# Residual kept in PSUM, norm scale applied to the gathered rows, one weight lent rows, fewer warm-up matmuls, last down weights by columns

## The chip, the core and the metric

The kernel runs on one core of a Trainium2 chip (trn2): TensorE (PE, with a separate weight-load stream PEld), VectorE (DVE), ScalarE (ACT), GpSimd (POOL), the queue of SyncE (SP) that issues nearly all transfers, and 16 DMA engines. The metric is the device time of one execution in microseconds; lower is better.

## What is computed

A trunk of two layers for 256 tokens of 1024 channels, all in float32. Layer 0 mixes by attention, layer 1 by a gated linear recurrence; behind each mixer stands a mixture of 32 SwiGLU experts, and a norm ends the trunk. Cut to what matters:

```python
for layer in range(2):
    h = h + mixer(rms_norm(h, norm_mix[layer]))
    x = rms_norm(h, norm_ffn[layer])
    # top-1 of 4 groups, then top-2 of the group's 8 experts; combine[s, e] is the weight or 0
    hid = silu(einsum('sd,edf->sef', x, w_gate)) * einsum('sd,edf->sef', x, w_up)
    h = h + einsum('sef,efd->sd', hid * combine[..., None], w_down)
return rms_norm(h, final_norm)
```

All 32 experts of a layer are computed, each on the tokens that chose it, so that 3 x 32 weight matrices of 1 MB are read in each layer.

## The kernel before

**Tiles.** The tokens are two row tiles t of 128. `h` is [128, 2, 1024] in SBUF, `xg` and `xT` are as large, `psum` has 8 banks of 512 floats. Weights lie in `ring` (6 slots of 16 KB a partition), in the `arena`, in `ahead`, and in rows lent for a time (`gain`, `xT`'s upper half as `y_rows`).

**Expert stage.** The experts go in 8 quads of 4. Every quad has at most 32 tokens an expert, so a quad fills the 128 columns of a matmul, each expert its own 32. For quad n TensorE does, in this order, in `body`: `gather` (16 matmuls, `xg` times the 0/1 matrix `slots`, so the chosen tokens come out transposed), `combine` of quad n-2 (4 matmuls of 512 columns that bring the quad's outputs back to the token rows, times `shareT`), `turn_hidden` of n-1, `later_gate_up` of n (32 matmuls; the four experts of a step run side by side), `down` of n-1 (16 matmuls) and `turn_shares`. ACT and DVE copy the gathered rows out of PSUM (ACT the front half in four pieces, DVE the back half, L1558), compute silu, and copy the down product to `y_rows`. DVE adds the four banks of each combine to `h` (`add_rows`, L1549). ACT writes `xg` as h times the norm's `rstd` once per layer (`scaled_rows`). Quad 0 uses pieces of its gate/up weights (`first_gate_up`, four pieces c) as they come; the first lies between the two halves of the gather.

**Transfers.** SP issues them in program order and stands at each wait. `later_quad(n, q, parity, ended)` waits until gate/up of quad n-2 is done (its slots are free), issues the 8 gate and up matrices of quad q, waits for the down product of quad n-2 and issues the 4 down matrices of the quad `ended`. So quad 3's eight loads (L500) wait for gate/up of quad 1, and quad 2's down loads (L508) for the down product of quad 1 and everything ahead of it on TensorE. The last quad's down weights (`load_last_down`, L541) come in four transfers: row half j = 0 of both slots, then j = 1.

**Ends.** Behind the last quad, ACT squares h by halves (`norm_by_halves`), DVE norms both tiles (L1246), and in layer 0 the transposes, the split in high and low parts and the products of the recurrence follow; in layer 1 two stores do. At the start `keep_clock(16, 7)` issues 16 matmuls on the identity (L1816), the gain row is spread by two matmuls (L1822), eight more follow, and then come the norm's transposes (L1798).

## Time and profile before

| | us |
|---|---|
| median of 3 runs | 728.1 |
| lowest, highest | 727.38, 729.61 |
| the profiled execution | 732.78 |
| its span, first to last instruction | 731.1 |
| TensorE busy in it | 624.0 (85%) |
| DVE, ACT busy in it | 300.8, 242.6 |
| moved by DMA | 244.52 MB, mean 334 GB/s |

The span is a little shorter than its execution's time. Busy shares are means over stages that differ: the slices and windows show them apart. In a timeline row the columns are start, duration, engine, line, operation, out and in tiles, shape, count of records, and in brackets the idle time ahead and what ended it. A float32 matmul shows as two records (a transpose as one), and its records overlap, so that the start-to-start distance tells the pace.

### The profile page before, as it was taken

To read this page: it belongs to the slowest core of one execution; us is meant where nothing else is said; L and a number is where in the kernel's file an instruction comes from. 1 tells how busy PE (TensorE), PEld (TensorE's weight loads), DVE (VectorE), ACT (ScalarE), POOL (GpSimd) and SP (SyncE) were. 2 spreads that over 40 slices of the span, in tenths; PEclk is the share of its full clock that TensorE was granted. 3 is DMA by queue.
4 is the path that set the end of the run, shared out by engine and by line. 5 is a ranking of instruction groups with operands and counts; after the bars stand their busy time and mean duration, and the time that the engine had idled before them with its cause. 6 is when DMAs were issued, how large, how long until landed. Compare 5 with 4: busy or idle time off the path is not lost.

```text
span 731.1 us, 11097 instructions
## 1 busy us (share of the span) xinstructions
PE 624.0 (85%) x4490; PEld 411.3 (56%) x4490; DVE 300.8 (41%) x518; ACT 242.6 (33%) x540; POOL 35.2 (5%) x64
## 2 busy tenths in 40 slices
PE   8999899999997595675989999999999976595775
PEld 7997787776542341322269987887754431341321
DVE  3756687524232211312285698652522330221304
ACT  4545556442211110100157685662411110110112
POOL 3020000000000100000000001060000000000000
PEclk9999999999999888977999999999999998897989
DMA  8949336799999999999996636579989999999993
GB/s 325 274 123 340 114 117 208 306 403 360 401 422 392 410 420 421 421 422 422 405 388 220 231 128 218 185 265 403 386 358 392 416 422 422 422 421 421 421 415 142
DMA packets 59712, 244.52 MB, mean 334 GB/s; under 512 B 4545, under 2 KB 8913, under 8 KB 38930
## 3 DMA queue, kind: packets, MB, share of 16 engines
q1 hardware_dynamic: 58400, 242.33, 84.5%
q0 software_dynamic: 768, 1.40, 0.8%
q8 instruction: 31, 0.51, 0.3%
q10 hardware_dynamic: 498, 0.15, 0.1%
q14 instruction: 15, 0.12, 0.0%
HBM read 242.82 MB, written 1.05 MB: 334 GB/s over the span
## 4 chain that ended last, share of the span: by engine, by line
PE 54%; DMA 31%; DVE 5%; SPq 5%; ACT 2%; issue 2%; DVEq 0%; POOL 0%; POOLq 0%; ACTq 0%
DMA ring<-in_moe_w_down 31%; PE psum L2278 7%; PE psum L1849 6%; PE psum L2223 6%; PE psum L1860 3%; PE psum L1853 3%; SPq L541 3%; PE psum L1851 3%; PE psum L1858 3%; PE psum L2216 3%; PE psum L2358 2%; PE psum L2360 2%; PE psum L2359 2%; SPq L508 2%; PE psum L1816 1%
## 5 line engine op out<-in xcount | busy, mean ns | idle before, releaser
L2223 PE MATMUL psum<-ring,xT 128*32 128x512 f32 x512 | 66.9, 679 | 33.5 <-DMA ring<-in_moe_w_up 33.5
L2223 PE MATMUL psum<-arena,xT 128*32 128x512 f32 x512 | 63.9, 657 | 34.6 <-DMA arena<-in_moe_w_up 34.6
L1567 DVE TENSOR_TENSOR arena<-psum,arena 128x256 f32<-128x256 f32 x16 | 6.8, 425 | 210.3 <-ACT arena L1051 210.3
L2278 PE MATMUL psum<-ring,arena 128*32 128x512 f32 x456 | 61.8, 626 | 14.4 <-DMA ring<-in_moe_w_down 14.3
L1047 ACT ACTIVATE arena<-psum 128x256 f32<-128x256 f32 x16 | 6.1, 383 | 202.0 <-PE psum L2223 202.0
L2216 PE MATMUL psum<-arena,xg 128*128 128x128 f32 x512 | 61.5, 277 | 0.8 <-DVE arena L1553 0.8
L2216 PEld LDWEIGHTS psum<-arena,xg 128*128 128x128 f32 x512 | 59.3, 193 | 2.7 <-issue 2.7
L2223 PEld LDWEIGHTS psum<-arena,xT 128*32 128x32 f32 x512 | 16.9, 120 | 76.8 <-issue 41.2
L2223 PEld LDWEIGHTS psum<-ring,xT 128*32 128x32 f32 x512 | 16.9, 123 | 76.0 <-issue 41.1
L2207 PE MATMUL psum<-xT,arena 128*128 128x512 f32 x128 | 57.7, 594 | 0.0
L1849 PE MATMUL psum<-x_hi,w_hi 128*128 128x256 f32 x224 | 56.0, 288 | 1.7 <-DVE x_hi L1252 1.2
L1549 DVE TENSOR_TENSOR h<-psum,h 128x512 f32<-128x512 f32 x64 | 44.2, 690 | 9.3 <-PE psum L2207 8.2
L1853 PE MATMUL psum<-x_hi,w_lo 128*128 128x256 f32 x192 | 47.0, 283 | 0.0
L2278 PEld LDWEIGHTS psum<-ring,arena 128*32 128x32 f32 x456 | 15.6, 114 | 53.3 <-issue 36.1
L1849 PEld LDWEIGHTS psum<-x_hi,w_hi 128*128 128x128 f32 x224 | 42.7, 191 | 3.6 <-issue 1.8
L835 ACT ACTIVATE w_hi<-ring 128x1024 fp32r<-128x1024 f32 x32 | 32.7, 1052 | 18.7 <-PE psum L1860 11.6
L2207 PEld LDWEIGHTS psum<-xT,arena 128*128 128x128 f32 x128 | 23.1, 190 | 24.6 <-issue 24.6
L410 DVE TENSOR_TENSOR w_lo<-ring,w_hi 128x1024 fp32r<-128x1024 f32 x28 | 33.3, 1220 | 8.5 <-ACT w_hi L835 8.5
L1853 PEld LDWEIGHTS psum<-x_hi,w_lo 128*128 128x128 f32 x192 | 36.7, 191 | 0.0
L1860 PE MATMUL psum<-x_lo,w_hi 128*128 128x256 f32 x224 | 31.5, 283 | 0.1
L1558 DVE TENSOR_TENSOR xT<-psum,gain_ffn 128x512 f32<-128x512 f32 x16 | 11.1, 692 | 46.3 <-PE psum L2216 46.3
L1040 ACT ACTIVATE xT<-psum,gain_ffn 128x128 f32<-128x128 f32 x64 | 18.5, 367 | 31.8 <-PE psum L2216 31.8
(341 smaller groups left out, 1050.2 us busy)
## 6 DMA issues: line engine op xcount, KB each, us to landing
ring<-in_moe_w_down SPq DMA_DIRECT2D x54, 1024.0 KB, 20.1
ring<-in_moe_w_gate SPq DMA_DIRECT2D x32, 1024.0 KB, 15.5
ring<-in_moe_w_up SPq DMA_DIRECT2D x32, 1024.0 KB, 17.7
arena<-in_moe_w_gate SPq DMA_DIRECT2D x32, 1024.0 KB, 20.7
arena<-in_moe_w_up SPq DMA_DIRECT2D x32, 1024.0 KB, 22.6
ring<-in_rec_w_in SPq DMA_DIRECT2D x16, 1024.0 KB, 13.7
ring<-in_att_w_in SPq DMA_DIRECT2D x8, 1024.0 KB, 10.7
ring<-in_att_w_out SPq DMA_DIRECT2D x4, 1024.0 KB, 14.7
```

Source lines behind the costliest of these rows:

```text
L410: eng.tensor_tensor(quarter_lo(base, r), quarter(base, r), quarter_hi(r).bitcast(F32), ALU.subtract)\
L541: sp.dma_start(slot.rearrange("p (e j n) -> p e j n", e=2, j=KF)[:, :, j, :], v[j][:, 2 * i:2 * i + 2, :])\
L835: act.activation(quarter_hi(r), quarter(base, r), ACT.Copy).then_inc(s["w_high"], 1)
L1549: dve.tensor_tensor(v, bank(b), v, ALU.add).then_inc(done, 1)
L1849: pe.matmul(dst, a_hi(k), b_hi(k), start=(k == 0), stop=False)
L1851: pe.matmul(dst, a_hi(k), b_lo(k), start=False, stop=False)
L1853: pe.matmul(dst, a_lo(k), b_hi(k), start=False, stop=False)
L1860: last = pe.matmul(dst, a_hi(k), b_lo(k), start=False, stop=(k == KD - 1))
L2207: pe.matmul(bank(b), shareT[:, t, :], y_rows[:, half * 512:(half + 1) * 512], start=True, stop=True).then_inc(s[f"combined{l}"], 1)
L2216: last = pe.matmul(gather_bank(k, first)[:, k % 4 * P:(k % 4 + 1) * P], xg_parts[:, t, k, :], slots[:, t].rearrange("p e c -> p (e c)"), s ...
L2223: return pe.matmul(bank(3)[e * CAP:(e + 1) * CAP, :].rearrange("p (w f) -> p w f", w=2), gatheredT[:, k, e * CAP:(e + 1) * CAP], w, start= ...
L2278: last = pe.matmul(bank(5 + c)[e * CAP:(e + 1) * CAP, :], hidT[:, j, e * CAP:(e + 1) * CAP], down_part(l, kind, e, j)[:, c * 512:(c + 1) * ...
```

## The change

1. **Sums in PSUM.** `combine` accumulates in banks 0 to 3 over all quads; DVE's `add_rows` is gone. In the body of quad 2 `start_sums` first writes h there, by four matmuls with the identity. The working banks move to 4 to 7. At the layer's end norm and squares read PSUM; in layer 0 h is copied back to SBUF later.
2. **Scale after the gather.** `scaled_rows` is gone; `gather` reads h itself, with a step of 8 floats, and adds two matmuls of one column that gather `rstd`. ACT copies that column negated (`slot_rate`), and silu uses it as a scale.
3. **Lent rows.** `xg` is free during the stage, so the gate matrix of quad 2's expert 0 is loaded there during the mixer (`load_in_x`); its expert's product is split in two matmuls of 256 columns.
4. **Quad 0** does pieces 0 and 1 of gate/up between the halves of the gather.
5. **Warm-up.** `START, FIRST` go from 16, 4 to 6, 2; the identity is made before the ones.
6. **Last quad.** Its down weights come in eight transfers, by column half and then row half; TensorE takes them in that order, and combines the front columns ahead of the last piece.
7. **Between the layers** the small lower-bound work moves ahead of the last down product; the first product of the recurrence takes its three parts one after the other; the last store is in two halves.

```diff
+LAST_PARTS = ((0, 0, "last_down_front"), (0, 1, "last_down_front"), (1, 0, "rest_loaded"), (1, 1, "last_down_back"))
...
+        def load_in_x(sp, l, *free):
+            sp.wait_ge(*free)
+            sp.dma_start(x_weights, moe_w_gate[l].rearrange("(q e) (p r) f -> q e p (r f)", e=QE, p=P)[2][0])\
+                .then_inc(s[f"gate_up_loaded{l}_0"], 16)
...
-            for j in range(KF):
+            for c, j, done in LAST_PARTS:
                 for i, slot in enumerate(down_slots(l, True)):
-                    sp.dma_start(slot.rearrange("p (e j n) -> p e j n", e=2, j=KF)[:, :, j, :],
-                                 v[j][:, 2 * i:2 * i + 2, :])\
-                        .then_inc(s["last_down_back" if j else "last_down_front"], 16)
+                    sp.dma_start(slot.rearrange("p (e j n) -> p e j n", e=2, j=KF)[:, :, j, c * 512:(c + 1) * 512],
+                                 v[j][:, 2 * i:2 * i + 2, c * 512:(c + 1) * 512]).then_inc(s[done], 16)
...
                     load_lent(sp, 0, 0, s["xg_done"], TT)
+                    load_in_x(sp, 0, s["proj_psum"], 12)
...
-                    load_gate_up(sp, l, 2, 0, e)
+                    load_gate_up(sp, l, 2, 0, e, (0, 1) if e else (1,))
...
-        START, FIRST, ROUTE, NORM = 16, 4, 19, 10
+        START, FIRST, ROUTE, NORM = 6, 2, 19, 10
...
+            def slot_rate(l, n, parity, small=False):
+                act.wait_ge(s[f"rate_psum{l}"], n + 1)
+                act.activation(rate[:, parity:parity + 1], rate_psum(small), ACT.Copy, scale=-1.0)\
+                    .then_inc(s[f"gatheredT{l}"], 1)
...
-            def add_rows(l, m, done):
-                dve.wait_ge(s[f"added{l}"], 4 * m + 4)
-                for i, b in enumerate(COMBINE_BANKS):
-                    half, t = divmod(i, 2)
-                    v = h[:, t, half * 512:(half + 1) * 512]
-                    dve.wait_ge(s[f"combined{l}"], 4 * m + i + 1)
-                    dve.tensor_tensor(v, bank(b), v, ALU.add).then_inc(done, 1)
...
+            def start_sums(l):
+                for done in (f"y_front{l}", f"y_back{l}", "passes_ready"):
+                    pe.wait_ge(s[done], l + 1 if done == "passes_ready" else 1)
+                for half, t in SUM_TILES:
+                    pe.matmul(sum_bank(half, t), ident[:, :], h[:, t, half * 512:(half + 1) * 512],
+                              start=True, stop=False, skip_group_check=True)
...
-                    pe.matmul(bank(b), shareT[:, t, :], y_rows[:, half * 512:(half + 1) * 512],
-                              start=True, stop=True).then_inc(s[f"combined{l}"], 1)
+                    pe.matmul(sum_bank(half, t), shareT[:, t, :], y_rows[:, half * 512:(half + 1) * 512],
+                              start=False, stop=last, skip_group_check=True)\
+                        .then_inc(s["h_done" if last else f"combined{l}"], 1)
...
+                    if k == KD - 1:
+                        for t in range(TT):
+                            col = pe.matmul(rate_psum(small), slots[:, t].rearrange("p e c -> p (e c)"),
+                                            norm_rstd[:, v, t:t + 1], start=(t == 0), stop=(t == TT - 1))
+                        col.then_inc(s[f"rate_psum{l}"], 1)
...
+                        if in_x and e == 0:
+                            for i, part in enumerate((lent, w[0][:, 1])):
+                                pe.matmul(bank(GATE_UP)[0:CAP, i * FF:(i + 1) * FF], gatheredT[:, k, 0:CAP],
+                                          part[:, k, :], start=(k == 0 and i == 0), stop=(k == KD - 1),
+                                          skip_group_check=True)
...
-                down(l, end, last_quad=True)
-                pe.wait_ge(s[f"added{l}"], 4 * end + 4)
-                combine(l, end)
+                last_down(l, 0, 0)
+                last_down(l, 0, 1)
+                last_down(l, 1, 0)
+                combine(l, end, last=True, halves=(0,))
+                last_down(l, 1, 1)
+                combine(l, end, last=True, halves=(1,))
```

How TensorE's instructions stand, at three places. **Quad 0 of layer 0**, before; `arena` is `slots` (and hidden rows), `xT` the gathered tokens, `ring` the weights:

```order
L2216 MATMUL psum<-arena,xg 128x128 [waits slots0,route_exp,xg_done]
L2216 MATMUL psum<-arena,xg 128x128 x7
L2223 MATMUL psum<-ring,xT 32x512 [waits first_loaded0,first_front]
L2223 MATMUL psum<-ring,xT 32x512 x7
L2216 MATMUL psum<-arena,xg 128x128 x8
L2223 MATMUL psum<-ring,xT 32x512 [waits first_loaded1,first_front]
L2223 MATMUL psum<-ring,xT 32x512 x7
L2223 MATMUL psum<-ring,xT 32x512 [waits first_loaded2,gatheredT0]
L2223 MATMUL psum<-ring,xT 32x512 x7
L2223 MATMUL psum<-ring,xT 32x512 [waits first_loaded3,gatheredT0]
L2223 MATMUL psum<-ring,xT 32x512 x7
```

and after:

```order
L2276 MATMUL psum<-arena,h 128x128 [waits slots0,route_exp,norm_rstd]
L2276 MATMUL psum<-arena,h 128x128 x7
L2284 MATMUL psum<-ring,xT 32x512 [waits first_loaded0,first_front]
L2284 MATMUL psum<-ring,xT 32x512 x7
L2284 MATMUL psum<-ring,xT 32x512 [waits first_loaded1,first_front]
L2284 MATMUL psum<-ring,xT 32x512 x7
L2276 MATMUL psum<-arena,h 128x128 x6
L2272 MATMUL psum<-norm_rstd,arena 128x1 x2
L2276 MATMUL psum<-arena,h 128x128 x2
L2284 MATMUL psum<-ring,xT 32x512 [waits first_loaded2,gatheredT0]
L2284 MATMUL psum<-ring,xT 32x512 x7
L2284 MATMUL psum<-ring,xT 32x512 [waits first_loaded3,gatheredT0]
```

The second pair of gate/up rows now stands ahead of the gather's back half, and two matmuls on `norm_rstd` inside that half. **The body of quad 2 of layer 0**, from the gather to the start of gate/up, before:

```order
L2216 MATMUL psum<-arena,xg 128x128 [waits slots0,added0]
L2216 MATMUL psum<-arena,xg 128x128 x15
L2207 MATMUL psum<-xT,arena 128x512 [waits y_front0,shareT0]
L2207 MATMUL psum<-xT,arena 128x512
L2207 MATMUL psum<-xT,arena 128x512 [waits gatheredT0,y_back0]
L2207 MATMUL psum<-xT,arena 128x512
L2258 MATMUL psum<-ident,arena 128x128 [waits hid0]
L2258 MATMUL psum<-ident,arena 128x128
L2223 MATMUL psum<-ring,xT 32x512 [waits gate_up_loaded0_0,gatheredT0]
L2223 MATMUL psum<-ring,xT 32x512 x31
```

and after (the last two rows and three of 512 columns on `ring` behind them come eight times):

```order
L2276 MATMUL psum<-arena,h 128x128 [waits slots0]
L2276 MATMUL psum<-arena,h 128x128 x13
L2272 MATMUL psum<-norm_rstd,arena 128x1 x2
L2276 MATMUL psum<-arena,h 128x128 x2
L2243 MATMUL psum<-h,ident 128x512 [waits passes_ready,y_back0,y_front0]
L2243 MATMUL psum<-h,ident 128x512 x3
L2257 MATMUL psum<-xT,arena 128x512 [waits y_front0,shareT0]
L2257 MATMUL psum<-xT,arena 128x512
L2257 MATMUL psum<-xT,arena 128x512 [waits gatheredT0,y_back0]
L2257 MATMUL psum<-xT,arena 128x512
L2310 MATMUL psum<-xg,xT 32x256 [waits gate_up_loaded0_0,gatheredT0]
L2310 MATMUL psum<-ring,xT 32x256
```

The four matmuls on `h,ident` are new between gather and combine, and the rows of expert 0 are two of 256 columns. **The last quad of layer 0**, from its down product on, before:

```order
L2278 MATMUL psum<-ring,arena 32x512 [waits last_down_front,hidT0]
L2278 MATMUL psum<-ring,arena 32x512 x7
L2278 MATMUL psum<-ring,arena 32x512 [waits last_down_back]
L2278 MATMUL psum<-ring,arena 32x512 x7
L2322 REGISTER_ALU
L2207 MATMUL psum<-xT,arena 128x512 [waits y_front0,shareT0,added0]
L2207 MATMUL psum<-xT,arena 128x512
L2207 MATMUL psum<-xT,arena 128x512 [waits y_back0]
L2207 MATMUL psum<-xT,arena 128x512
L1816 MATMUL psum<-ident 128x128 x10
```

and after:

```order
L2398 MATMUL psum<-ident,chosen 128x16 [waits lb_loaded]
L2334 MATMUL psum<-ring,arena 32x512 [waits last_down_front,hidT0]
L2334 MATMUL psum<-ring,arena 32x512 x3
L2334 MATMUL psum<-ring,arena 32x512 [waits last_down_front]
L2334 MATMUL psum<-ring,arena 32x512 x3
L2334 MATMUL psum<-ring,arena 32x512 [waits rest_loaded]
L2334 MATMUL psum<-ring,arena 32x512 x3
L2257 MATMUL psum<-xT,arena 128x512 [waits y_front0,shareT0]
L2257 MATMUL psum<-xT,arena 128x512
L2334 MATMUL psum<-ring,arena 32x512 [waits last_down_back]
L2334 MATMUL psum<-ring,arena 32x512 x3
L2257 MATMUL psum<-xT,arena 128x512 [waits y_back0,shareT0]
```

The product is in four pieces with a wait each, the front columns are combined ahead of the last piece, and the lower-bound transpose stands ahead of all.

## Rows read from the trace of the kernel before

**Rows 1.** The page's 40 slices of 18.3 us: TensorE's busy tenths, GB/s moved.
```profile
PE   8999899999997595675989999999999976595775
...
GB/s 325 274 123 340 114 117 208 306 403 360 401 422 392 410 420 421 421 422 422 405 388 220 231 128 218 185 265 403 386 358 392 416 422 422 422 421 421 421 415 142
```

**Rows 2.** The page's chain that ended last, by line, share of the span.
```profile
DMA ring<-in_moe_w_down 31%; PE psum L2278 7%; PE psum L1849 6%; PE psum L2223 6%; PE psum L1860 3%; PE psum L1853 3%; SPq L541 3%; PE psum L1851 3%; PE psum L1858 3%; PE psum L2216 3%; PE psum L2358 2%; PE psum L2360 2%; PE psum L2359 2%; SPq L508 2%; PE psum L1816 1%
```

**Rows 3.** Windows: stretch, length, busy us (count) by engine, PEclk, DMA share, GB/s.
```profile
135.20:140.20 5.00, 4.35 (x31) 3.15 (x30) 1.45 (x3) 2.94 (x4) 0.00 (x0) 1.00 0.14 38
...
197.20:197.80 0.60, 0.60 (x8) 0.60 (x7) 0.02 (x1) 0.57 (x3) 0.00 (x0) 1.00 0.70 232
...
197.80:216.00 18.20, 18.20 (x144) 8.75 (x144) 7.00 (x13) 4.04 (x11) 1.16 (x2) 1.00 1.00 414
...
529.20:532.20 3.00, 3.00 (x26) 1.45 (x19) 0.00 (x0) 0.00 (x0) 0.00 (x0) 0.84 0.21 41
...
555.00:573.00 18.00, 18.00 (x142) 8.55 (x142) 6.80 (x13) 3.84 (x11) 0.58 (x1) 1.00 0.99 412
```

**Rows 4.** Timeline of SP's DMA issues: start, us, line, what is loaded.
```profile
124.67 0.43 SPq L534 DMA_DIRECT2D gain<-in_moe_w_down  x1
...
196.62 0.35 SPq L500 DMA_DIRECT2D arena<-in_moe_w_gate  x1
...
214.64 1.88 SPq L508 DMA_DIRECT2D ring<-in_moe_w_down  x4
...
553.64 0.34 SPq L500 DMA_DIRECT2D arena<-in_moe_w_gate  x1
...
571.65 1.88 SPq L508 DMA_DIRECT2D ring<-in_moe_w_down  x4
```

**Rows 5.** Timeline, layer 0: transposes of h, counts, an eviction, gather, combine.
```profile
158.85 2.04 PE L1808 MATMUL psum<-ident,h 128*128 128x128 f32 x16
...
169.18 0.39 PE L2193 MATMUL psum<-member,ones 128*128 128x32 f32 x2
...
169.40 0.39 PE L2194 MATMUL psum<-member,ones 128*128 128x32 f32 x2
...
176.18 0.69 DVE L1558 TENSOR_TENSOR xT<-psum,gain_ffn 128x512 f32<-128x512 f32 x1 [2.75 <-PE psum L2216]
...
196.60 3.74 PE L2216 MATMUL psum<-arena,xg 128*128 128x128 f32 x32
...
200.18 3.60 PE L2207 MATMUL psum<-xT,arena 128*128 128x512 f32 x8
```

**Rows 6.** Timeline of the kernel's start.
```profile
1.86 6.72 PE L1816 MATMUL psum<-ident 128*128 128x128 f32 x32 [1.86 <-POOL eps_col L713]
...
8.51 1.98 PE L1822 MATMUL psum<-gain,ones 1*128 1x512 f32 x4
...
10.61 2.47 DVE L1240 SCALAR_TENSOR_TENSOR xg<-h,norm_rstd,psum 128x1024 f32<-128x1024 f32 x2 [10.61 <-PE psum L1822]
...
17.11 2.17 PE L1874 MATMUL psum<-x_hi,w_hi 128*128 128x256 f32 x16 [0.35 <-ACT w_hi L937]
```

**Rows 7.** Timeline, end of layer 0 (one row), then of layer 1.
```profile
371.80 2.48 DVE L1246 SCALAR_TENSOR_TENSOR xg<-h,norm_rstd,gain 128x1024 f32<-128x1024 f32 x2 [0.94 <-ACT norm_rstd L826]
...
715.65 1.92 PE L2278 MATMUL psum<-ring,arena 128*32 128x512 f32 x16
...
718.17 1.92 PE L2278 MATMUL psum<-ring,arena 128*32 128x512 f32 x16 [0.59 <-DMA ring<-in_moe_w_down]
...
719.30 0.60 ACT L1065 ACTIVATE xT<-psum 128x512 f32<-128x512 f32 x1 [3.16 <-PE psum L2278]
...
720.04 3.68 PE L2207 MATMUL psum<-xT,arena 128*128 128x512 f32 x8
...
724.07 0.63 ACT L814 ACTIVATE arena<-h 128x512 f32<-128x512 f32 x1
...
725.39 2.48 DVE L1246 SCALAR_TENSOR_TENSOR xg<-h,norm_rstd,gain 128x1024 f32<-128x1024 f32 x2 [0.94 <-ACT norm_rstd L826]
```

285 lines of the change are left out of this document (166 added, 119 removed).

## Prediction

> **What bounds the kernel now.** I read the 40 slices of the page first, then the chain that ended last, then the DMA share in windows of my own, then the timelines of the queue SP and of TensorE. The slices show two regimes [rows 1]: TensorE is at 9 tenths or more through both mixers and the first part of each expert stage, and from about 200 us (and again from about 550 us) the 16 DMA engines are at 9 tenths with about 420 GB/s while TensorE falls to 5 to 7 tenths. The chain agrees: 31% of the span is spent waiting for the down weights [rows 2]. The expert stages are therefore a race in which the transfers win in the end, and what counts is the moment from which the transfers never stop. The windows give that moment [rows 3]: the DMA share is 1.00 from 197.8 us in layer 0 and 0.99 from 555 us in layer 1, and the slices behind stay at some 420 GB/s [rows 1]. Before it there are holes: 135.2 to 140.2 (share 0.14), 197.2 to 197.8 (0.70), and 529.2 to 532.2 (0.21). From that moment on the end of a layer is fixed by bytes alone.
>
> What starts the last stretch is TensorE. The eight transfers of quad 3 are issued at 196.62 (553.64 in layer 1) as soon as the gate/up product of quad 1 is finished, and the down weights of quad 2 at 214.64 (571.65) as soon as the down product of quad 1 is finished [rows 4]. TensorE has no idle between the two: it is busy for 18.2 of the 18.2 us of that window [rows 3], with gather, combine [rows 5], gate/up and down back to back. Eight transfers are 8 x 1.05 MB = 8.4 MB; at the 414 GB/s of [rows 3] they take 20.3 us and run from 197.8 to 218.1. The next issue at 214.64 brings data some 1.3 us later (196.62 to 197.8 and 553.64 to 555.0 are the same delay), at 215.9. **So TensorE has 2.1 us of slack in layer 0**, and in layer 1, where data flow from 555.0 to 575.3 and the issue at 571.65 brings data at 573.0, 2.3 us. Whatever the change adds on TensorE before the end of quad 1's down product, beyond that slack, delays the layer's end one for one.
>
> **The change part by part.**
>
> *Work added on TensorE before that point.* (a) Each gather now carries two matmuls of one column. None is in the trace; the nearest rows are the count matmuls of 32 columns, 0.22 us from start to start (169.18 to 169.40), paced by their weight loads. Lower bound 0.1, upper 0.25 us each; I take 0.22, so 0.44 per gather and 1.3 us for the three gathers (0, 1, 2) before the point. (b) In quad 0 the second piece of gate/up moves ahead of the back half of the gather. DVE's eviction of that half (0.69 us [rows 5], starting 0.2 to 0.3 after the gather's end) was hidden behind that piece; now the third piece waits for it: about 0.95 us. (c) Before the sums, h is put in PSUM by four matmuls with 512 columns. Four such matmuls are the combine, 3.60 us for its eight records, 0.86 from start to start [rows 5]: 3.4 us. They stand between gather 2 and combine 0, where nothing was idle, so nothing hides them. (d) Quad 2's expert 0 is split in two matmuls of 256 columns, eight times. The columns are the same; experts run side by side. If only the pipeline skews, this costs one half step, 0.4 us; if every extra start held up the other experts it would cost 3.4 us; nothing in the trace has mixed widths. I take 0.4, because four experts overlap fully in every gate/up row. Sum: 1.3 + 0.95 + 3.4 + 0.4 = 6.1 us, minus the slack: **+4.0 us in layer 0 and +3.8 us in layer 1.** What is queued behind it is the SP queue: it stands at the wait for quad 1's down product and has 12 transfers behind that wait.
>
> *The lent rows.* One gate weight (1 MB, 2.5 us of transfer) is now issued behind the last transfer of its group at 124.67 [rows 4] and flows in the hole at 135.2 to 140.2 [rows 3], which is 5 us long; in layer 1 it moves likewise into mixer time. It costs nothing there. But it gains nothing either: it shortens the queue before the issue of quad 3, and that issue waits for TensorE. The queue runs dry at about 194.7 instead of 197.2 and idles longer. The bytes after the point are the same.
>
> *What is removed.* ACT's scaled copies (2.2 and 2.4 us) and DVE's four adds of 0.69 us per quad leave engines that are idle for half of these stages: worth nothing until the last quad. The extra waits on y_front and y_back before a gather are met: the copies end before TensorE has turned the shares. The small extra ACT instruction (0.2 us) is covered by combine.
>
> *Short warm-up.* Before, 32 warm-up records take 6.72 us (0.21 each, the lower clock), then the gain matmuls run from 8.51, DVE's first norm starts at 10.61, released by them and by nothing later, and the first product at 17.11 [rows 6]. With 6 instead of 16 the warm-up ends at about 4.1, the gain matmuls (1.98 us at the upper, twice that at the lower clock) end at about 8.0, so the norms start 2.5 us earlier, and the 8 warm-up matmuls that held back the transposes become 3. Against it: the transposes may run at the lower clock throughout (0.21 instead of 0.13 us each [rows 5, 6]). I take -2.4 us, with bounds -3.2 and -0.5 (the lower clock until the first products have run for some microseconds). The mixer is a chain of compute with holes in the DMA, so the shift arrives at the expert stage.
>
> *End of layer 0.* The sum stays in PSUM, the last down product comes by columns. TensorE is nearly the bound here. From 715.65 in layer 1 [rows 7] (layer 0 ends in the same pattern): three pieces of 0.86 us to 718.2; ACT copies the first half of the rows 1.13 us after the start of its second piece (718.17 to 719.30) in 0.60, so until 718.3; two combine matmuls to 720.1; the last piece, its copy, and combine at 722.0; the result 1.15 us later, the square and rstd 1.3 us (724.07 to 725.39), first final norm at 724.5. Before it was 725.39. So 0.9 us, although the last transfer now is followed by only a quarter of the product: TensorE itself is late. In layer 0 a small transpose costs 0.2 of it: the first norm at 371.0 instead of 371.80, and DVE, busy without a gap until the second product, passes 0.8 us on. The two copies of h to SBUF (2.4 us of DVE) take the place of 1.7 us for the lower bounds, 5 us before DVE is needed: nothing.
>
> The last 4 MB now come in rows of 2 KB. Slices with 2 KB rows (the projection weights, slices 20 and 21) show 405 and 388 GB/s against 421 [rows 1]: 0.3 to 0.8 us, hidden, since TensorE needs the last piece only at 720.1 and it had arrived at 718.17.
>
> *End of layer 1.* The same 0.9, then the second tile is normed and stored in halves: the last store is 256 KB, not 512. DVE ends 0.8 earlier and the store is some 0.3 shorter: -1.1 us.
>
> **Sum:** +4.0 + 3.8 - 2.4 - 0.8 - 1.1 = +3.5 us. The profiled execution took 732.8 us with a span of 731.1, 4.7 above the median of 728.1; I carry the difference over to the median: 731.5 us (a profile of it would show a span near 734.5).
>
> **A rule of the skill.** The gathers now read h with a step of 8 floats as the stationary operand, where xg was contiguous. The transposes of h already load such an operand (16 records in 2.04 us at 158.85), and the gather of contiguous xg takes 3.74 us for 32 [rows 5]: 0.12 us each, both. The Trainium skill, page "SBUF — State Buffer", section "Door 1: The DMA port swizzle (why `[64,N]` ≈ `[32,N]`)", says that each access that crosses to a new 16-byte line pays a penalty, so that only 4 floats of step are free. By that rule the gathers would slow down; the trace shows no such penalty for this operand.
>
> **The rivals.**
> - *The cover holds.* TensorE's 6.1 us stay behind the transfers, because quad 3's weights flow slower than I think or the wait in (b) vanishes. It decides at 2.1 us: below that, only the gains are left, -4.3 us, 723.8. For it speaks that the DMA share is 1.00 right up to 216 us; against it, (c) alone is 3.4 us and its price stands in a row. Chance 0.12, faster.
> - *The clock stays low at the start.* The warm-up gives back only 0.5 us: 733.4. For it speaks that the 32 records of the warm-up took 0.21 us each to their end, so that 12 of them will not have raised the clock; against it, that the transposes and the three matmuls behind the gain are dense work too. Chance 0.11, slower.
> - *Mixed widths hold up the experts:* (d) costs 3.4 and not 0.4, in both layers: 737.5. Chance 0.07.
> - *Steps in h cost:* if a stepped weight load took twice the time, three gathers would cost 3 x 3.6 us more in each layer, 753. The transposes speak against it. Chance 0.03.
> - *A lucky phase:* in layer 1 the first gate/up piece ran partly at the lower clock (granted share 0.84 in the hole at 529, 1.00 in layer 0's windows [rows 3]); if that falls away, -1.7, and with the start at its bound of -3.2 the sum is +1.0: 729.1. Chance 0.17, no difference.
>
> **How the numbers follow.** The forecast keeps 0.50, of which 0.10 lie within 0.3% of 728.1 (about 2.2 us, what a measurement of this kernel can tell from no change). Slower: 0.40 + 0.11 + 0.07 + 0.03 = 0.61; same: 0.10 + 0.17 = 0.27; faster 0.12. The range leaves out the cover that holds and the stepped loads, 0.15 in all, and takes in the mixed widths: 725.5 to 737.5; the forecast's own range is 729.5 to 734.
>
> **What would show it.** In the profile after: the issue of quad 3 at about 198.5 minus the start's gain and that of quad 2's down weights 22 us later (18.0 before); a hole of some 4 to 5 us in the DMA before the first and of 2 us before the second; four matmuls of 0.86 us on h and ident; gathers that have grown by 0.44 us; a first product near 14.7 us instead of 17.1. I am wrong if there is no hole after the down product of quad 1, or if the first product is not earlier.

## The result: 760.3 us, 4.2% slower, far outside the range

| | before | changed |
|---|---|---|
| median, us | 728.86 | 760.32 |
| lowest, highest | 727.38, 732.4 | 759.74, 762.65 |
| runs | 4 | 4 |
| span of the profiled execution | 731.1 | 757.6 |
| TensorE busy in it | 624.0 (85%) | 696.4 (92%) |

The ratio of the runs is 1.0424, 95% interval 1.0394 to 1.0453. The forecast was 731.5 us, the range 725.5 to 737.5. The page of the changed kernel, TensorE's busy tenths and GB/s of 40 slices of 18.9 us:

```profile
PE   9999899999999987977989999999999998977976
...
GB/s 327 258 206 342 36 132 323 348 407 303 203 362 324 402 421 421 421 421 423 392 387 229 189 201 144 266 328 408 305 320 278 280 415 421 422 421 420 422 410 169
```

Against [rows 1] TensorE is at 9 tenths or more in 29 slices, not 24, and the transfers fall to 203 GB/s in slice 11 (401 before) and to 305, 320, 278 and 280 in slices 29 to 32 (386, 358, 392 and 416 before). The gather's 512 records (L2216) were 61.5 us of TensorE before; now its line L2276 leads the page (TensorE, then its loads: count, busy us, mean ns):

```profile
L2276 PE MATMUL psum<-arena,h 128*128 128x128 f32 x512 | 129.7, 407 | 0.8 <-DVE arena L1588 0.8
...
L2276 PEld LDWEIGHTS psum<-arena,h 128*128 128x128 f32 x512 | 124.9, 334 | 2.7 <-issue 2.7
```

Timeline of TensorE in the body of quad 2 of layer 0, and two of SP's issues (start, us, engine, line):

```profile
203.01 6.85 PE L2276 MATMUL psum<-arena,h 128*128 128x128 f32 x28
...
209.70 0.51 PE L2272 MATMUL psum<-norm_rstd,arena 128*128 128x1 f32 x4
...
210.07 1.20 PE L2276 MATMUL psum<-arena,h 128*128 128x128 f32 x4
...
211.10 3.60 PE L2243 MATMUL psum<-h,ident 128*128 128x512 f32 x8
...
203.03 0.35 SPq L511 DMA_DIRECT2D arena<-in_moe_w_gate  x1
...
229.05 2.19 SPq L525 DMA_DIRECT2D ring<-in_moe_w_down  x4
```

The gather takes from 203.01 to 211.27, 8.26 us, where [rows 5] show 3.74. Each of its 32 records now starts 0.24 us behind the one ahead instead of 0.11. The rest is as foreseen: the one-column matmuls 0.4 to 0.5 us a gather, `start_sums` 3.60 us. The issue of quad 3 moved from 196.62 [rows 4] to 203.03, that of quad 2's down weights from 214.64 to 229.05. Windows (stretch, length, busy us of PE, PEld, DVE, ACT, POOL, PEclk, DMA share, GB/s) show what stands between:

```profile
198.75:204.25 5.50, 5.50 (x48) 2.55 (x40) 0.00 (x0) 1.31 (x4) 0.00 (x0) 1.00 0.15 22
...
224.50:230.50 6.00, 6.00 (x55) 3.14 (x46) 1.99 (x4) 1.90 (x4) 1.25 (x2) 1.00 0.12 23
...
230.50:250.00 19.50, 19.50 (x129) 11.19 (x132) 1.54 (x4) 3.28 (x10) 1.60 (x3) 1.00 0.99 390
...
596.00:602.00 6.00, 6.00 (x51) 3.20 (x44) 1.99 (x4) 1.90 (x4) 0.58 (x1) 1.00 0.13 23
```

TensorE is busy to the last microsecond of all four, the DMA engines stand nearly idle in the first two and the last (shares of 0.12 to 0.15), and from 230.5 on the transfers run without a gap. So the picture of the race was right, and TensorE lost it by much more than forecast. The whole kernel as a table of milestones, all from the timelines of TensorE (us from the span's start; G0 first gather, G3 start of quad 3's gather, which is the end of quad 1's down product and the point that lets the transfers run; D6 start of quad 6's down product, ' for layer 1). The differences in brackets are the length of a stretch against that of the kernel before:

| kernel | G0 | G3 | D6 | G0' | G3' | D6' | end |
|---|---|---|---|---|---|---|---|
| before | 170.2 | 214.6 | 354.3 | 525.6 | 571.6 | 708.0 | 731.1 |
| changed | 167.1 (-3.1) | 229.1 (+17.6) | 365.6 (-3.1) | 537.9 (+1.0) | 600.4 (+16.5) | 735.2 (-1.7) | 757.6 (-0.6) |
| e8_cover | 169.8 (-0.4) | 222.7 (+8.5) | 359.6 (-2.8) | 530.8 (-0.1) | 582.1 (+5.3) | 717.1 (-1.4) | 740.2 (0.0) |
| e9_copy | 167.1 (-3.1) | 219.1 (+7.6) | 356.5 (-2.3) | 528.5 (+0.7) | 578.9 (+4.4) | 714.0 (-1.3) | 736.4 (-0.7) |
| e4_scaled | 167.6 (-2.6) | 216.4 (+4.4) | 353.4 (-2.7) | 524.5 (-0.2) | 573.3 (+2.8) | 708.3 (-1.4) | 730.7 (-0.7) |
| e2_before_step | 170.1 (-0.1) | 226.7 (+12.2) | 363.6 (-2.8) | 534.7 (-0.2) | 591.6 (+10.9) | 726.4 (-1.6) | 749.5 (0.0) |
| e11_layer1 | 167.8 (-2.4) | 230.2 (+18.0) | 367.1 (-2.8) | 539.4 (+1.0) | 589.8 (+4.4) | 724.6 (-1.6) | 747.0 (-0.7) |
| e5_late | 167.0 (-3.2) | 213.1 (+1.7) | 351.5 (-1.3) | 522.4 (-0.4) | 568.4 (0.0) | 704.8 (0.0) | 727.3 (-0.6) |
| e6_start | 166.9 (-3.3) | 211.4 (+0.1) | 350.1 (-1.0) | 521.2 (-0.2) | 567.2 (0.0) | 703.5 (-0.1) | 726.6 (0.0) |
| e7_last | 170.0 (-0.2) | 214.4 (0.0) | 353.1 (-1.0) | 525.1 (+0.7) | 569.5 (-1.6) | 705.9 (0.0) | 729.8 (+0.8) |
| e12_cover2 | 167.5 (-2.7) | 213.7 (+1.8) | 351.2 (-2.2) | 522.3 (-0.2) | 568.5 (+0.2) | 703.6 (-1.3) | 726.6 (-0.1) |
| e10_best | 167.0 (-3.2) | 211.5 (+0.1) | 349.4 (-1.8) | 520.1 (-0.6) | 564.5 (-1.6) | 701.2 (+0.3) | 723.5 (-0.8) |

The trace's 26.5 us are 17.6 + 16.5 in the stretches that hold gathers 0 to 2, less 3.1 and 1.7 behind them and 2.7 at the start, the transition and the end together. The medians differ by 31.5, 5 more, because the profiled execution of before, with 732.8 us, was a little longer than the longest of its four runs here; a part of the spread is traced below.

### The profile page after: what moved, and what is told of

Read it like the earlier page. It is cut to its first block, busy times and chain, and to the rows that moved or that the text cites. A ratio compares the mean times of both kernels' runs of the same rounds, so it can differ in the third digit from the quotient of the medians.

```text
span 757.6 us, 11143 instructions
## 1 busy us (share of the span) xinstructions
PE 696.4 (92%) x4568; PEld 486.3 (64%) x4568; DVE 262.6 (35%) x457; ACT 237.7 (31%) x552; POOL 35.1 (5%) x64
## 4 chain that ended last, share of the span: by engine, by line
PE 66%; DMA 25%; DVE 5%; issue 2%; SPq 1%; ACT 1%; DVEq 0%; POOL 0%; POOLq 0%; ACTq 0%
DMA ring<-in_moe_w_down 25%; PE psum L2276 8%; PE psum L2353 7%; PE psum L2284 7%; PE psum L1878 6%; PE psum L2257 4%; PE psum L1882 3%; PE psum L1889 3%; PE psum L1880 3%; PE psum L1887 3%; PE psum L2440 2%; PE psum L2441 2%; PE psum L2442 2%; SPq L525 1%; PE psum L1844 1%
## 5 line engine op out<-in xcount | busy, mean ns | idle before, releaser
L2276 PE MATMUL psum<-arena,h 128*128 128x128 f32 x512 | 129.7, 407 | 0.8 <-DVE arena L1588 0.8
L2276 PEld LDWEIGHTS psum<-arena,h 128*128 128x128 f32 x512 | 124.9, 334 | 2.7 <-issue 2.7
L1604 DVE SCALAR_TENSOR_TENSOR arena<-psum,arena 128x256 f32<-128x256 f32 x16 | 7.7, 484 | 211.1 <-ACT arena L1079 211.1
L2284 PE MATMUL psum<-ring,xT 128*32 128x512 f32 x480 | 63.8, 656 | 13.4 <-DMA ring<-in_moe_w_up 11.6
L2353 PE MATMUL psum<-ring,arena 128*32 128x512 f32 x392 | 52.5, 613 | 8.7 <-DMA ring<-in_moe_w_down 8.4
L1075 ACT ACTIVATE arena<-psum,arena 128x256 f32<-128x256 f32 x16 | 7.6, 473 | 150.7 <-PE psum L2284 150.7
L1878 PE MATMUL psum<-x_hi,w_hi 128*128 128x256 f32 x216 | 54.2, 289 | 0.7 <-issue 0.3
L1882 PE MATMUL psum<-x_hi,w_lo 128*128 128x256 f32 x184 | 45.3, 284 | 0.0
L2353 PEld LDWEIGHTS psum<-ring,arena 128*32 128x32 f32 x392 | 13.4, 112 | 40.3 <-issue 24.2
L1889 PEld LDWEIGHTS psum<-x_lo,w_hi 128*128 128x128 f32 x216 | 27.8, 192 | 0.0
## 6 DMA issues: line engine op xcount, KB each, us to landing
ring<-in_moe_w_up SPq DMA_DIRECT2D x32, 1024.0 KB, 14.3
ring<-in_moe_w_down SPq DMA_DIRECT2D x22, 512.0 KB, 11.7
```

Of the source, the lines that this page charges most:

```text
L1878: pe.matmul(dst, a_hi(k), b_hi(k), start=(k == 0), stop=False)
L1882: pe.matmul(dst, a_lo(k), b_hi(k), start=False, stop=False)
L1889: last = pe.matmul(dst, a_hi(k), b_lo(k), start=False, stop=(k == KD - 1))
L2276: last = pe.matmul(gather_bank(k, first)[:, k % 4 * P:(k % 4 + 1) * P], h[:, t, :].rearrange("p (j k) -> p k j", k=KD)[:, k, :], slots[:, ...
L2284: return pe.matmul(bank(GATE_UP)[e * CAP:(e + 1) * CAP, :].rearrange("p (w f) -> p w f", w=2), gatheredT[:, k, e * CAP:(e + 1) * CAP], w, ...
L2353: last = pe.matmul(down_bank(c, first)[e * CAP:(e + 1) * CAP, :], hidT[:, j, e * CAP:(e + 1) * CAP], down_part(l, kind, e, j)[:, c * 512:( ...
```

## The experiments

**Theory S:** the step of 8 floats in the loaded operand of the gather is what costs, and everything else is as forecast. **Theory R:** something else in the new stage slows the gather (its PSUM banks, its waits, the tile h). **Theory C**, for the terms besides: the end of quad 1's down product is what lets the transfers run, with some 2 us of cover in each layer (cover: how long the transfers already issued still last when TensorE reaches that point). In what follows "us by the ratio" means the ratio of a kernel's runs to those of the kernel before in the same session, times 730; it is what the intervals belong to. In three chip sessions the kernel before had medians of 730.3 (13 runs: e1 to e4), 729.56 (29: e5 to e8) and 728.06 (23: e9 to e12).

### The step of 8

`e1_packed` changes one operand of the changed kernel:

```diff
-                                         h[:, t, :].rearrange("p (j k) -> p k j", k=KD)[:, k, :],
+                                         h[:, t, k * P:(k + 1) * P],
```

> The changed kernel, but each gather reads 128 neighbouring channels of h (128 floats in a row) instead of every eighth one. So it gathers the wrong channels; instructions, waits and bytes are the same. Theory S (the step of 8 floats in the loaded operand is what costs): the gather goes back from 8.1 us to 3.74 + 0.44 = 4.2 us, three gathers ahead of the transfers' last start fall by 3.9 each in both layers, and the time falls from 760.3 by some 23 to 26 us, to 734 to 737, near what the other steps of the prediction give. Theory R (something else in the new stage costs it: the other PSUM banks, the new waits, h in place of xg): the gather stays at 8.1 us and the time at 760.

Its time (975.46 us) says nothing: with other channels in h after layer 0 the routing of layer 1 is another, so that a second round of quads runs there. It counts 768 records of the gather where the changed kernel counts 512. Layer 0 is as it was, and its timeline of quad 2 reads:

```profile
195.99 3.29 PE L2276 MATMUL psum<-arena,h 128*128 128x128 f32 x28
...
199.11 0.50 PE L2272 MATMUL psum<-norm_rstd,arena 128*128 128x1 f32 x4
...
199.48 0.69 PE L2276 MATMUL psum<-arena,h 128*128 128x128 f32 x4
...
200.01 3.60 PE L2243 MATMUL psum<-h,ident 128*128 128x512 f32 x8
```

From 195.99 to 200.17, 4.18 us, against 8.26 with the same banks, waits, tile and count: R is out. `e11_layer1` makes the same edit in layer 1 alone, so that its time can be read:

> The changed kernel with the gathers of layer 1 alone reading 128 neighbouring channels of h (wrong channels in layer 1, so that the routing of both layers is as it should be; instructions, waits and bytes unchanged). Theory S: layer 0 as in the changed kernel, in layer 1 three gathers less 3.9 us each ahead of the transfers' last start: 11.7 us less, 748.6. Theory R: 760.

748.83 us (747.87 to 749.32, 4 runs): 11.5 us less than the changed kernel, which ran in another session (10.8 by the two ratios, 1.0424 and 1.0276); 11.7 were expected. And the same edit the other way round, in the kernel before:

```diff
-                        last = pe.matmul(gather_bank(k, first)[:, k % 4 * P:(k % 4 + 1) * P], xg_parts[:, t, k, :],
+                        last = pe.matmul(gather_bank(k, first)[:, k % 4 * P:(k % 4 + 1) * P],
+                                         xg[:, t, :].rearrange("p (j k) -> p k j", k=KD)[:, k, :],
```

> The kernel before, but the gather reads xg with a step of 8 floats (so the wrong channels), all else untouched. Theory S: each gather grows by 4.1 us, three stand ahead of the transfers' last start, 2.1 and 2.3 us of that are covered: 12.3 - 2.1 and 12.3 - 2.3, so +20 us, 749. Theory R: no change, 729.

750.28 us (749.44 to 751.18, 4 runs; ratio 1.0278, 1.024 to 1.0316), the forecast to 1.3 us. Its gather of quad 2:

```profile
204.57 7.81 PE L2216 MATMUL psum<-arena,xg 128*128 128x128 f32 x32
```

So one access pattern, alone, puts 20 us on the kernel before. Last, one that computes the full result: `e9_copy` is the changed kernel, ACT copies h packed into xg (which gives up the lent rows):

```diff
+            def packed_rows(v, t):
+                act.wait_ge(s["norm_rstd"], TT * v + t + 1)
+                act.activation(xg_parts[:, t], h[:, t, :].rearrange("p (j k) -> p k j", k=KD), ACT.Copy)\
+                    .then_inc(s["xg_done"], 1)
...
-                                         h[:, t, :].rearrange("p (j k) -> p k j", k=KD)[:, k, :],
+                                         xg_parts[:, t, k, :],
```

> The changed kernel with one thing of its part 2 undone: ACT copies h packed (unscaled) into xg and the gather reads that, so the lent rows (part 3) fall away too; the one-column matmuls and all else stay. It computes the full result. Theory S: the gathers take 3.74 + 0.44 us as in e1_packed, and the whole 26 us between the changed kernel and e4_scaled go but for the one-column matmuls: e4's 734.2 plus 2 x 3 x 0.44 = 2.6, so 736.8. If the step were only part of the cause, it stays above 740.

736.45 us (734.7 to 738.11, 4 runs): 24 of the 31 us are gone with one copy on an idle engine. It is 2.25 us above e4_scaled by the medians and 3.1 by the ratios, which fits the one-column matmuls, forecast at 2.6.

### What a step costs, and why the trace of before seemed to say it is free

> The kernel before with another step in every gather (wrong channels): layer 0 has steps of 1, 2, 4, 8 floats in quads 0 to 3, then 16 and 3 by turns; layer 1 has quads 0 and 1 with the operands swapped (the 0/1 matrix loaded, xg streamed, steps 1 and 8), then 6, 5, and 12 and 7 by turns. The transposes of h in layer 1 are made by an ordinary product with h (step 8) loaded and the identity streamed. If lines of 16 bytes set the price of the loaded operand, steps 1 and 2 take 3.74 us, 4 and more take the same 8.1 us or 4 is free too and the jump lies behind it; if the price grows with the step, 16 costs more than 8 and 12 more than 6. If only the loaded operand pays, the swapped gather with step 8 takes 3.74 us; if the streamed one pays too, it grows as well. If the transposes of h load the identity and stream h, as I now suppose, the ordinary product in layer 1 takes 0.25 us a record, against 0.128 of the transposes in layer 0.

`e3_steps` is the kernel before with `xg` read flat, `flat[:, k:k + 127 * step + 1:step]`, another step in each quad. Its gathers on TensorE, in order of time: step 2 (two halves of 16 records, one shown), 4, 8, 16 and 3 in layer 0, then in layer 1 the swapped operands with step 8 (one half), and steps 6, 5, 12 and 7:

```profile
181.19 2.06 PE L2228 MATMUL psum<-arena,xg 128*128 128x128 f32 x16
...
196.34 7.63 PE L2228 MATMUL psum<-arena,xg 128*128 128x128 f32 x32
...
218.27 7.78 PE L2228 MATMUL psum<-arena,xg 128*128 128x128 f32 x32
...
240.35 7.15 PE L2228 MATMUL psum<-arena,xg 128*128 128x128 f32 x32
...
269.27 5.76 PE L2228 MATMUL psum<-arena,xg 128*128 128x128 f32 x32
...
544.83 3.89 PE L2228 MATMUL psum<-xg,arena 128*128 128x128 f32 x16
...
563.31 7.29 PE L2228 MATMUL psum<-arena,xg 128*128 128x128 f32 x32
...
584.90 7.26 PE L2228 MATMUL psum<-arena,xg 128*128 128x128 f32 x32
...
606.46 8.75 PE L2228 MATMUL psum<-arena,xg 128*128 128x128 f32 x32
...
634.75 7.58 PE L2228 MATMUL psum<-arena,xg 128*128 128x128 f32 x32
```

| step, floats | 1 | 2 | 3 | 4 | 5 | 6 | 7 | 8 | 12 | 16 |
|---|---|---|---|---|---|---|---|---|---|---|
| start to start of a record, us | 0.112 | 0.118 | 0.175 | 0.233 | 0.222 | 0.223 | 0.232 | 0.238 | 0.268 | 0.218 |

The price is flat to step 2, at 3 it is half way, at 4 the full one, and behind that it hardly grows. That is 0.233 us times the number of 16-byte lines an element touches (a half at step 2, three quarters at step 3: 0.175, one from 4 on), with a floor of 0.112. That sum is fitted to these rows, and from 5 on they leave it by up to 15%, without order: 16 is the cheapest (0.218), 12 the dearest (0.268). Why was not tried. The Trainium skill, page "SBUF — State Buffer", section "Door 1: The DMA port swizzle (why `[64,N]` ≈ `[32,N]`)", asks for two hits in each line of 16 bytes; this ladder agrees. The same paragraph goes on that 4 floats of step are free; here 4 floats cost the full price, 7.63 us for 32 records against 4.12 with 2.

With the operands swapped (the 0/1 matrix loaded, xg streamed) 16 records take 2.05 us packed and 3.89 with a step of 8, 0.233 us each. So it isn't a matter of the loaded operand alone; my expectation left that open. Nor do long load records go with the slow pace there (PEld, swapped, step 8; count, busy us, mean ns):

```profile
L2228 PEld LDWEIGHTS psum<-xg,arena 128*128 128x128 f32 x10 | 2.1, 209 | 0.2
```

The price also hangs on TensorE's clock. In the changed kernel a stretch of 3.4 us at the lower clock (1.2 GHz) fell on the first gather, in the kernel before one began within the front half of layer 1's first. Sixteen stepped records at the lower and at the full clock, then sixteen packed ones with the lower clock from about the tenth on, then the windows of the first and the third row:

```profile
167.07 4.12 PE L2276 MATMUL psum<-arena,h 128*128 128x128 f32 x16 [0.42 <-DVE arena L1588]
...
183.91 3.98 PE L2276 MATMUL psum<-arena,h 128*128 128x128 f32 x16
...
525.59 2.68 PE L2216 MATMUL psum<-arena,xg 128*128 128x128 f32 x16 [0.42 <-DVE arena L1553]
...
167.10:171.10 4.00, 4.00 (x16) 3.84 (x16) 2.67 (x16) 0.62 (x2) 0.00 (x0) 0.57 0.87 335
...
525.60:528.20 2.60, 2.60 (x16) 2.38 (x17) 2.19 (x13) 0.62 (x2) 0.00 (x0) 0.72 1.03 418
```

At the lower clock a packed record starts 0.214 us behind the one ahead (0.112 at the full clock), a stepped one 0.240 (0.238). So the step doubles a record's time at 2.4 GHz and adds about a tenth at 1.2 GHz.

The prediction dismissed the rule on the transposes of h, which read the same tile with the same step at 0.128 us a record, the pace of the packed gather. `e3_steps` turns h in layer 1 by an ordinary product with the identity. The two, one behind the other:

```profile
158.47 2.04 PE L1812 MATMUL psum<-ident,h 128*128 128x128 f32 x16
...
514.67 7.88 PE L1810 MATMUL psum<-ident,h 128*128 128x128 f32 x32
```

Sixteen transposes take 2.04 us, sixteen ordinary products of the same operands (two records each) 7.88. So the transposes were a true row that answered another question. (A record names the streamed operand first, as the swapped gather `xg,arena` shows; both rows here read `ident,h`. So by its name a transpose loads h, and my guess in the expectation that it streams h was wrong, though the time it gave came out.) The trace of before held a warning that I passed over: the transposes' own loads. Load records on PEld, of the norm's packed xg (L1798) and of h (L1808): count, duration in ns min/median/max:

```profile
L1798 PEld LDWEIGHTS psum<-ident,xg x32: 138/141/230, 13.0 to 375.1; 128*128 128x128 f32 x32
...
L1808 PEld LDWEIGHTS psum<-ident,h x32: 185/190/207, 158.8 to 515.9; 128*128 128x128 f32 x32
```

The load of the stepped operand is 50 ns longer. In a transpose it hides: records of both kinds follow each other every 0.109 us, but for the first few of a group. In the gather the load records grew from 192 to 334 ns (the L2276 row above). That the next record waits for its load would explain that case, but not the swapped one, whose loads take 209 ns at nearly the same pace; so the mechanism inside TensorE stays open. Why a transpose bears the step better than a product was not tried.

### The cover, and the terms ahead of it

`e8_cover` and `e12_cover2` put idle work into the kernel before, in the body of quad 2:

```diff
+                if early:
+                    for i in range(8):   # 2 in e12_cover2
+                        pe.matmul(bank(7), ident[:, :], h[:, i % 2, 0:512], start=True, stop=True)
                 combine(l, n - 2, gathers=n)
```

> The kernel before with eight matmuls of 512 columns on the identity between gather and combine of quad 2, whose result nobody reads: 6.9 us of TensorE ahead of the transfers' last start in each layer. Theory C: 6.9 less the cover of 2.1 and 2.3 is +4.8 and +4.6, so +9.4 us, 739.7. If there is no such cover it is +13.8; if it is larger than 6.9, no change.

> As e8_cover with two matmuls in place of eight: 1.7 us of TensorE ahead of the transfers' last start in each layer. By the prediction's cover of 2.1 and 2.3 us nothing is left, no change, 729.6; without cover it is +3.4, 733.

e8: 741.88 us (740.01 to 741.97, 4 runs), ratio 1.0154 (1.0112 to 1.0196), so +11.2 of the 13.8 us put in, with an interval of 8.2 to 14.3; e12: 731.06 us (727.36 to 733.97, 10 runs), ratio 1.0028 (1.0001 to 1.0056), so +2.0 of 3.4, where none was expected. In layer 1 of e8:

```profile
560.75 7.03 PE L2291 MATMUL psum<-h,ident 128*128 128x512 f32 x16
...
582.08 3.74 PE L2216 MATMUL psum<-arena,xg 128*128 128x128 f32 x32
```

The work stands ahead of G3' in full, and behind it the stretch to D6' is shorter by what the transfers had in hand: 1.4 us in layer 1. In layer 0 the stretch from G3 to D6 is 136.9 us, where the kernels that add nothing ahead of G3 (e5, e6, e7, e10) have 137.9 to 138.7: 1.0 to 1.8 us. (The profiled execution of before, with 139.7, was 1 us long there, so the -2.8 of the table is too much.) Cover in both layers is then 2.4 to 3.2 us by the traces and 2.6 by the ratio of e8 (its interval alone would allow -0.5 to 5.6), where the forecast had 4.4. e12's trace agrees: its stretches to D6 and D6' are 0.4 to 1.2 and 1.3 us shorter; its ratio would say 1.4, with an interval of 4 us.

`e4_scaled` undoes parts 2 and 3 of the change, `e5_late` also moves h's way into the sums to the body of quad 3 and brings quad 0 back to its old order:

```diff
-                if early:
-                    start_sums(l)
-                combine(l, n - 2, gathers=n)
+                combine(l, n - 2, gathers=n, first=early)
+                if sums:
+                    start_sums(l)
```

> The changed kernel with its parts 2 and 3 undone: ACT writes xg scaled and packed, the gather reads that, no one-column matmuls, no lent rows; sums in PSUM, the order of quad 0, the short warm-up, the last quad and the transition stay. Theory S and the prediction's terms: what is left ahead of the transfers' last start is 0.95 + 3.4 = 4.4 us less 2.1 and 2.3, so +2.3 and +2.1, less 2.4, 0.8 and 1.1: 729, about no change. Theory R: if the PSUM sums or the order are what costs, it stays above 745.

> As e4_scaled, but h is added into the PSUM sums in the body of quad 3, ahead of its gate/up, where TensorE waits for transfers, and quad 0 again has only its first piece between the halves of the gather. The first combine starts the sums. So nothing is left ahead of the transfers' last start. Theory C (that point and its cover of 2.1 and 2.3 us decide): e4's 4.4 us a layer go, 2.3 and 2.1 of them uncovered, so 4.4 us faster than e4: 729.8 by its 734.2, and the DMA hole behind the down product of quad 1 (0.75 us in e4) is gone. Rival N (e4's 4 us come from elsewhere, the last quad or the start): this stays at 734.

e4: 734.2 us (732.46 to 735.75, 8 runs), ratio 1.0058 (1.0031 to 1.0085), 4.2 us slower where about none was expected: 1.9 of it is the smaller cover, 1.2 the end (see below), the rest not traced; e5: 727.3 us (725.35 to 730.83, 12 runs), ratio 0.9966 (0.9943 to 0.9989). So 6.9 us between them (6.7 by the ratios), where 4.4 were expected: 2 x 4.4 us of TensorE less a cover of 2.5 gives 6.3. In the timeline the four matmuls on h stand behind quad 3's combine now (575.45, 3.60 us), and D6' does not move: the same work costs its 3.4 us, less what cover is left, ahead of G3 and nothing behind it.

### The start, the last quad, and the spread

> The kernel before with the short warm-up alone (6 and 2 for 16 and 4, identity before the ones). Prediction: 2.4 us faster, 727.9 by the 730.3 before, bounds -3.2 and -0.5. Rival: the earlier start shifts when the clock falls and rises in the layers behind, and takes the gain back: no change or slower, though the first gather starts 3 us earlier.

`e6_start` (the numbers 6 and 2 and the order of the two constants in the kernel before): 726.92 us (725.52 to 728.86, 12 runs), ratio 0.9954 (0.9932 to 0.9975), 3.4 us faster by the ratio, 1.8 to 5.0. Its first product and gain matmuls, against 17.11 and 8.51 in [rows 6]:

```profile
4.46 3.78 PE L1823 MATMUL psum<-gain,ones 1*128 1x512 f32 x4
...
9.69 3.52 PE L1798 MATMUL psum<-ident,xg 128*128 128x128 f32 x16
...
13.80 2.21 PE L1875 MATMUL psum<-x_hi,w_hi 128*128 128x256 f32 x16 [0.15 <-DVE x_lo L1260]
```

The gain matmuls and the first transposes do run at the pace of the lower clock, as feared (3.78 us against 1.98 [rows 6], 3.52 for 16 where 16 at the full clock take 2.04 [rows 5]), and still the first product is 3.3 us earlier, all of it kept to the expert stage (G0, -3.3). But one trace of each is not enough here. e12_cover2 has the long warm-up of the kernel before, e11_layer1 the short one, and their first products are:

```profile
14.20 2.17 PE L1874 MATMUL psum<-x_hi,w_hi 128*128 128x256 f32 x16 [0.34 <-ACT w_hi L937]
...
12.10 2.16 PE L1915 MATMUL psum<-x_hi,w_hi 128*128 128x256 f32 x16
```

So the start alone moves by up to 2.9 us from one execution to another with the same instructions. With the long warm-up the traces have 14.2 and 16.6 to 17.1, with the short one 12.1 and 13.8 to 13.9: early against early the gain is 2.1 us, late against late 2.7 to 3.3. Nor is an early start always kept: e11_layer1 has another stretch at the lower clock at 25.7, and its G0 is -2.4. The forecast of 2.4 is not refuted.

> The kernel before with the last quad's down weights in eight transfers by column halves alone, and the down product and combine in that order (DVE still adds the sums to h). Prediction: 0.9 us earlier at the end of each layer, 1.8 us faster in all, 728.5. Rival: rows of 2 KB slow the last 4 MB (0.3 to 0.8 us), and the fourth piece, DVE's copy and the combine behind it now stand in a row: no gain.

`e7_last` (the loads and the product of the last quad as in the change's diff, DVE still adding): 731.4 us (728.35 to 734.33, 12 runs), ratio 1.0023 (0.9997 to 1.005). No gain: a loss of 1.7 us by the ratio, from -0.2 to 3.7, so not clear of none. Its end, and the same of the changed kernel:

```profile
713.54 2.78 PE L2202 MATMUL psum<-ring,arena 128*32 128x512 f32 x24
...
716.27 1.96 PE L2220 MATMUL psum<-xT,arena 128*128 128x512 f32 x4
...
718.17 1.06 PE L2202 MATMUL psum<-ring,arena 128*32 128x512 f32 x8
...
720.14 1.95 PE L2220 MATMUL psum<-xT,arena 128*128 128x512 f32 x4 [0.91 <-DVE xT L1573]
```

```profile
742.76 2.78 PE L2334 MATMUL psum<-ring,arena 128*32 128x512 f32 x24
...
747.39 1.07 PE L2334 MATMUL psum<-ring,arena 128*32 128x512 f32 x8
...
749.36 1.95 PE L2257 MATMUL psum<-xT,arena 128*128 128x512 f32 x4 [0.91 <-DVE xT L1612]
```

The first fence is e7_last, the second the changed kernel. In both TensorE idles 0.91 us between the fourth piece and the last combine, for DVE's copy of the rows. Before, the two pieces of the second row half stood behind the last transfer and the copies ran beside them, with a wait of 0.59 [rows 7]. And the loads are slower: the windows from 710 to 714, where both kernels have these transfers in flight:

```profile
710.00:714.00 4.00, 4.00 (x25) 1.70 (x18) 1.38 (x2) 0.98 (x2) 0.00 (x0) 1.00 1.03 411
```

```profile
710.00:714.00 4.00, 4.00 (x15) 1.51 (x17) 2.75 (x5) 0.74 (x2) 0.00 (x0) 1.00 1.05 387
```

The first is before, with 411 GB/s and rows of 4 KB, the second e7_last, with 387 and rows of 2 KB. That is 0.6 us for the 4.2 MB, inside the forecast's 0.3 to 0.8, and it stays hidden: no piece in the two fences above waits for a transfer.

> As e5_late (short warm-up, sums in PSUM with h added in quad 3, packed scaled rows, new transition), but the last quad's down weights and product as before, by row halves in four transfers; the combine behind it still ends in PSUM. If the column halves cost what e7_last shows alone (+1.7 us), this is 727.3 - 1.7 = 725.6, the fastest so far. If they cost nothing once DVE's adds are gone, it stays at 727.3 or is slower.

`e10_best` takes e5_late with the old last quad: 727.5 us (725.22 to 729.34, 12 runs), ratio 0.999 (0.9974 to 1.0006); against 727.3 of e5 nothing that can be told. From D6' to the end it takes 22.3 us, e5 22.5, the changed kernel 22.4, and the kernel before 23.1. So what shortens the end, by 0.6 to 0.8 us, is in e10_best too, most likely the sums in PSUM (no adds of 0.69 us behind the last combine); the column halves add nothing to it.

Two stretches of equal work show another part of the spread between executions, beside the start. From G0' to G3' there are 370 records in both, in the kernel before (first) and in e10_best:

```profile
525.60:571.60 46.00, 45.84 (x370) 22.27 (x371) 12.85 (x37) 9.46 (x27) 0.00 (x0) 0.96 0.93 378
```

```profile
520.10:564.50 44.40, 44.24 (x370) 21.55 (x371) 10.19 (x33) 9.48 (x27) 0.00 (x0) 1.00 0.96 389
```

The granted clock was 0.96 in one and 1.00 in the other: in the kernel before the end of the first half gather and a part of the first gate/up piece fell into a stretch at 1.2 GHz (526.8 to 530.2) behind TensorE's idle time of the routing, in e10_best none did. The same 1.6 us make the odd entries of the table: e8_cover's stretch took 52.9 us in layer 0 at 0.97 and 51.3 in layer 1 at 1.00, e9_copy's 52.0 at 0.97 and 50.4 at 1.00. This is the phase that the prediction's fifth rival spoke of; it stands in traces of either kind, so that it belongs to the run and not to the change. The changed kernel had such a stretch in both layers (0.97), where it cost little, since it fell on stepped records. Executions of the kernel before differ by up to 6.8 us (726.37 to 733.15 in one session); what decides on which side one falls is not shown. A difference of 2 or 3 us between single traces says nothing for that reason.

## Where the prediction was right and wrong

- **What bounds the kernel: right.** The end of quad 1's down product lets the transfers run, TensorE is without idle time ahead of it, and work placed there costs almost its whole length (e8_cover), work behind it nothing (e5_late). The cover of 2.1 and 2.3 us was too large: the traces show 1.0 to 1.8 and 1.4.
- **The gather's step: wrong, and it is 24 of the 29 us between forecast and result.** The step that failed is the paragraph on the rule: "0.12 us each, both ... the trace shows no such penalty for this operand". It set a transpose's record beside a product's, as if one cleared the other, and so put the step's price at nothing. The price was 4.1 us a gather, so 12.3 a layer, 24 in all with nothing left to cover it. The rival "Steps in h cost" had the mechanism and nearly the size (3.6 us a gather, 753 us; with 4.1 it is 756, and 760.3 was measured), but a chance of 0.03 and a place outside the range. What I called the transposes' evidence against it was a row of another kind of instruction. That the forecast named the right direction is no merit of this step: without the step the change is slower too (e9_copy), by 7.4 us where 3.5 was forecast.
- **The other added work: right.** One-column matmuls 0.44 a gather (0.4 to 0.5); `start_sums` 3.44 (3.60 us of records); the eviction wait in quad 0 0.95 (0.85); the split expert 0.4 was too much: gate/up of quad 2 took 7.0 us from its start to that of the down product (218.29 to 225.25), 6.9 before, so mixed widths cost nothing and that rival is out. The sum of them is 5.7 us a layer. With it in both layers, the start's -3.4, a cover of 2.5 in all and +1.0 for the last quad and the end (e7_last's +1.7 less the end's 0.7), e9_copy should be 6.5 us slower than before; it is 7.4 (ratio 1.0101, 1.007 to 1.0131, so 5.1 to 9.6). The +1.7 is not clear of none; without it the sum is 4.8.
- **Lent rows: right in that they gain nothing.** In layer 1 of e11_layer1 (with them) and of e9_copy (without) the stretch from G0' to G3' is 50.4 us in both, and the one to D6' 134.8 and 135.1.
- **The start: right in sign;** 3.4 us by the ratio (1.8 to 5.0), 2.1 to 3.3 by traces of like start, against 2.4. The rival that the clock stays low there was half right: it did, and the gain came all the same.
- **End of layer 0 and the transition:** the stretch D6 to G0' was +0.7 to +1.0 in the changed kernel, e9 and e11 (each with one stretch of 3.4 us at the lower clock in it), -0.2 to -0.6 in e4, e5 and e10: near nothing, where -0.8 was forecast.
- **End of layer 1, -1.1:** -0.6 to -0.8, most likely from the sums in PSUM. The column halves gave nothing, and the store in halves nothing either (from the first norm at 751.84 to the end 5.8 us, 5.7 before).
- **The median:** the span's difference carried over to the median misses 5 us here, since the one profiled execution of before was a long one; its trace has 1.6 us of that from the lower clock in layer 1's quad 0 and 1 us between G3 and D6.

## What to carry to other kernels

Before TensorE reads a tile with a step, ask how many 16-byte lines an element touches: up to 2 floats of step a float32 product of TensorE ran at nearly full pace, from 4 on it took twice the time, and a packed copy on an idle engine buys that back (24 us here). A row of the trace excludes a cost only if it is the same kind of instruction with the same bottleneck; where a written rule speaks against the change and the row is of another kind, price the rule in earnest. Look at more than one execution before a gain of 2 or 3 us at the start is read off a trace. And find the point that lets the transfers run: the same 3.4 us of matmuls cost nothing one quad later.

## What was unexpected of the hardware

- An ordinary float32 product of 128 x 128 takes 0.112 us a record packed, 0.118 with a step of 2 floats, 0.175 with 3, 0.22 to 0.24 with 4 to 8, 0.268 with 12 and 0.218 with 16, whether the loaded or the streamed operand has the step (8 was tried in both).
- At the lower clock (1.2 GHz) the packed record takes 0.214 us and the one with a step of 8 takes 0.240, against 0.112 and 0.238 at the full clock.
- Transposes of the same operand with a step of 8 keep their pace of 0.109 us a record, though their loads take 190 ns instead of 141.
- Matmuls of 256 and 512 columns, mixed among four experts side by side, cost nothing over 512 columns alone (7.0 us for gate/up of quad 2, 6.9 before).
- Weights in rows of 2 KB came at 387 GB/s where rows of 4 KB had 403 to 411.
